# The u units of a gating stage: three 256-column products per weight block, or one of 512 columns and one of 256

## The reference

```python
def chunked_sgu(h, w_in, ln_g, ln_b, w_s, b_s, w_out):
    z = jax.nn.gelu(h @ w_in)
    u, v = jnp.split(z, 2, axis=-1)
    v = layer_norm(v, ln_g, ln_b)
    v = v.reshape(B, nc, CHUNK, N_SGU_GROUPS, SGU_GROUP_DIM)
    ws = jnp.where(causal[None], w_s, jnp.zeros_like(w_s))
    sv = jnp.einsum("gts,bcsgd->bctgd", ws, v) + b_s.T[None, None, :, :, None]
    return (u * sv.reshape(B, S, SGU_HALF)) @ w_out
```

## Time and profile before

| what | value |
| --- | --- |
| times of three executions | 1108.13, 1108.94, 1110.29 us; median 1108.94 us |
| the profiled execution | 1108.64 us, span from first to last instruction 1106.5 us |
| PE busy | 1074.8 us (97%) |
| DVE, ACT, POOL busy | 781.8 us (71%), 642.5 us (58%), 96.8 us (9%) |
| chain that ended last | PE 86%, DVE 8%, ACT 3%, issue 2% |
| L173, L174, L175 with 256 columns | 1152 each |

### The profile page before, as it was taken

How to read it: one execution, slowest core, us unless ns; L and a number is a source line. 1 busy time by engine, 2 the same in 40 slices (tenths; PEclk the granted TensorE clock), 3 DMA queues, 4 the chain that set the end, 5 groups by cost and what they waited for, 6 DMA issues and landing times.

```text
span 1106.5 us, 20061 instructions
## 1 busy us (share of the span) xinstructions
PE 1074.8 (97%) x6870; PEld 949.7 (86%) x6870; DVE 781.8 (71%) x1331; ACT 642.5 (58%) x1158; POOL 96.8 (9%) x119
## 2 busy tenths in 40 slices
PE   8989999999999999999999999999999998999998
PEld 7967999999788998777999999899678887888886
DVE  6657877777654367886877777698779748666664
ACT  6658444444764855666444444677777747554443
POOL 0140111111010002220111111000100000000000
PEclk9999999999999999999999999999999999999999
DMA  9353665555366475442665555265212544555541
GB/s 340 103 197 113 224 195 184 197 190 191 114 247 199 125 228 171 153 152 77 213 203 190 189 192 190 77 221 180 96 39 71 175 155 154 190 188 190 190 152 38
DMA packets 51380, 185.06 MB, mean 167 GB/s; under 512 B 5728, under 2 KB 6240, under 8 KB 51328
## 3 DMA queue, kind: packets, MB, share of 16 engines
q1 hardware_dynamic: 49248, 178.28, 48.4%
q0 software_dynamic: 1504, 5.44, 1.4%
q10 hardware_dynamic: 576, 0.64, 0.2%
HBM read 183.29 MB, written 1.05 MB: 167 GB/s over the span
## 4 chain that ended last, share of the span: by engine, by line
PE 86%; DVE 8%; ACT 3%; issue 2%; DMA 0%; DVEq 0%; SPq 0%; ACTq 0%
PE ps L228 28%; PE ps L173 15%; PE ps L175 15%; PE ps L174 15%; PE ps L198 5%; DVE w_lo L156 3%; PE ps L200 2%; PE ps L1612 1%; ACT both L430 1%; DVE arena L815 1%; DVE both L436 1%; PE ps L750 1%; PE ps L734 1%; PE ps L721 1%; PE ps L1623 1%
## 5 line engine op out<-in xcount | busy, mean ns | idle before, releaser
L156 DVE TENSOR_TENSOR w_lo<-raw,w_hi 128x1024 fp32r<-128x1024 f32 x336 | 418.0, 1254 | 118.5 <-ACT w_hi L151 116.7
L151 ACT ACTIVATE w_hi<-raw 128x1024 fp32r<-128x1024 f32 x336 | 346.9, 1052 | 98.8 <-PE ps L175 51.3
L173 PE MATMUL ps<-both,w_hi 128*128 128x256 f32 x1152 | 328.0, 285 | 1.9 <-DVE both L436 0.9
L174 PE MATMUL ps<-both,w_hi 128*128 128x256 f32 x1152 | 326.2, 283 | 0.0
L175 PE MATMUL ps<-both,w_lo 128*128 128x256 f32 x1152 | 326.2, 283 | 0.0
L228 PE MATMUL ps<-w_hi,both 128*128 128x512 f32 x992 | 293.8, 396 | 7.3 <-DVE both L1197 3.3
L173 PEld LDWEIGHTS ps<-both,w_hi 128*128 128x128 f32 x1152 | 221.1, 192 | 6.2 <-issue 2.9
L174 PEld LDWEIGHTS ps<-both,w_hi 128*128 128x128 f32 x1152 | 221.2, 192 | 1.5
L175 PEld LDWEIGHTS ps<-both,w_lo 128*128 128x128 f32 x1152 | 221.1, 192 | 0.0
L228 PEld LDWEIGHTS ps<-w_hi,both 128*128 128x128 f32 x992 | 178.8, 188 | 45.6 <-DVE w_lo L156 4.3
L228 PE MATMUL ps<-w_lo,both 128*128 128x512 f32 x496 | 158.2, 392 | 0.0
(11 more groups left out here) (199 smaller groups left out, 1095.8 us busy)
## 6 DMA issues: line engine op xcount, KB each, us to landing
raw<-in_w SPq DMA_DIRECT2D x336, 512.0 KB, 3.4
row<-in_rows POOLq DMA_DIRECT2D x7, 512.0 KB, 4.2
x<-in_x SPq DMA_DIRECT2D x2, 512.0 KB, 4.4
out<-x SPq DMA_DIRECT2D x4, 256.0 KB, 2.1
misc<-in_misc POOLq DMA_DIRECT2D x1, 512.0 KB, 5.7
arena<-in_ws POOLq DMA_DIRECT2D x1, 512.0 KB, 7.7
tab<-in_tables POOLq DMA_DIRECT2D x1, 320.0 KB, 4.4
tab<-in_tables POOLq DMA_DIRECT2D x1, 256.0 KB, 4.6
```

The lines of the kernel that those rows point to most:

```text
L151: act.activation(w_hi[:, s, :], raw[:, s, :], ACT.Copy).then_inc(hi_done, 1)
L156: dve.tensor_tensor(w_lo[:, s, :], raw[:, s, :], w_hi[:, s, :].bitcast(F32), ALU.subtract).then_inc(lo_done, 1)
L173: pe.matmul(o, l_hi, r_hi, start=first, stop=False)
L174: pe.matmul(o, l_hi, r_lo, start=False, stop=False)
```

## The change

- `features_apart` takes the place of `features` for the 24 units of u. The ring is now of single units: unit m fills bank `UB = (7, 0, 3)[m % 3]`, so three banks hold three units.
- Behind each unit, ACT copies the bank's second half to the buffer `pad` (L1095), DVE adds it to the first half and writes the sum to `G_U` (L1161, counted by `u_summed`). PE takes the bank again after that sum. Behind each pair, DVE multiplies the two sums by `ROW` in `G_U` (L1167), and ACT applies the gelu in place there (L1099). The weight splits stand between these steps: ACT copy, hi, copy, hi, gelu; DVE add, lo, add, multiply, lo.
- The 12 squares are four, three, three and two, with pairs 0, 1 and 2 between them. The root and its table load follow the last two, then an explicit load of the gelu table, then pair 3. The normalisations vn of tiles 0 to 2 move behind pair 8, and their spatial matmuls on PE from ahead of unit 18 to ahead of unit 20.
- Output tile 0 no longer waits for all gelus: its first token tile (banks 0 and 1) waits for the sum of unit 22, its second (banks 2 and 3) for that of unit 23. On ACT the second `high` stands before pair 11, on DVE the second `low` too.

```diff
-    UB = (7, 0, 1)
+    UB = (7, 0, 3)
...
-        for p in range(3):
-            if p == 1:
-                pe.wait_ge(g_sem.v, 2 * SGC)
-            for k in range(2):
-                features(pe, N_SGU + 2 * p + k, ps[:, UB[p], k * SEQ:(k + 1) * SEQ])
-        def later_pair(p, i=0):
-            pe.wait_ge(g_sem.u, p - 2 + 3 * i)
-            for k in range(2):
-                features(pe, N_SGU + 2 * p + k, ps[:, UB[p % 3], k * SEQ:(k + 1) * SEQ], i)
...
+        def u_unit(m, i=0):
+            if m in (1, 2):
+                pe.wait_ge(g_sem.v, 8)
+            if m >= 3:
+                pe.wait_ge(g_sem.u_summed, m - 2 + 6 * i)
+            features_apart(pe, N_SGU + m, UB[m % 3], i)
...
-        out_tile(0)
+        pe.wait_ge(g_sem.lo, 1)
+        for tt in range(TT):
+            pe.wait_ge(g_sem.u_summed, SGT - 1 + tt)
+            accumulate(pe, N_SGO, s_slot(0), True, False, tiles=(tt,))
...
         def pair(p, i, split):
-            split(0)
+            for k in range(2):
+                m = 2 * p + k
+                act.wait_ge(unit_used, N_SGU + m + 1 + 6 * i)
+                if m >= 2:
+                    act.wait_ge(g_sem.u_summed, m - 1 + 6 * i)
+                act.activation(pad[:, k, 2:2 + SEQ], ps[:, UB[m % 3], SEQ:2 * SEQ], ACT.Copy).then_inc(g_sem.u_part, 1)
+                split(k)
             act.wait_ge(g_sem.u_scaled, p + 1 + 3 * i)
-            dst = G_U[:, 2 * p:2 * p + 2, :] if isinstance(i, int) else G_U[:, bass.ds(2 * p + 6 * i, 2), :]
-            act.activation(dst.rearrange("p a b -> p (a b)"), ps[:, UB[p % 3], :],
-                           ACT.Gelu_apprx_tanh).then_inc(g_sem.u, 1)
-            split(1)
+            u = u_pair(p, i).rearrange("p a b -> p (a b)")
+            act.activation(u, u, ACT.Gelu_apprx_tanh).then_inc(g_sem.u, 1)
...
-        moments(0)
+        moments(0, 4)
         straight_pair(0)
-        moments(1)
+        moments(4, 7)
         straight_pair(1)
+        moments(7, 10)
+        straight_pair(2)
+        moments(10, 2 * SGC)
         act.wait_ge(g_sem.stat, 4)
         act.activation(lns[:, L_ROOT:L_ROOT + 2], lns[:, L_VAR:L_VAR + 2], ACT.Sqrt).then_inc(g_sem.root, 1)
-        act.wait_ge(g_sem.stat, 6)
-        for j in range(3):
-            vn(j)
-        straight_pair(2)
+        act.preload_act_table(ACT.Gelu_apprx_tanh)
...
-        def pair_row(p, i=0):
-
-            dve.wait_ge(unit_used, N_SGU + 2 * p + 2 + 6 * i)
-            uv = ps[:, UB[p % 3], :].rearrange("p (k t) -> p k t", k=2)
-            dve.tensor_tensor(uv, uv, ROW.rearrange("p (a t) -> p a t", a=1).to_broadcast([P, 2, SEQ]),
+        def pair_row(p, i=0, split=lambda j: None):
+            for k in range(2):
+                m = 2 * p + k
+                dve.wait_ge(g_sem.u_part, m + 1 + 6 * i)
+                dve.tensor_tensor(u_one(m, i), ps[:, UB[m % 3], 0:SEQ], pad[:, k, 2:2 + SEQ],
+                                  ALU.add).then_inc(g_sem.u_summed, 1)
+                if k == 0:
+                    split(0)
+            dve.wait_ge(g_sem.u_summed, 2 * p + 2 + 6 * i)
+            u = u_pair(p, i)
+            dve.tensor_tensor(u, u, ROW.rearrange("p (a t) -> p a t", a=1).to_broadcast([P, 2, SEQ]),
                               ALU.mult).then_inc(g_sem.u_scaled, 1)
+            split(1)
```

More of the change, by code:

```diff
@@ L971, in build @@
     L_SUM, L_SQ, L_TOT, L_NEG, L_VSUM, L_VAR, L_ROOT, L_INV, L_SHIFT = 0, 12, 24, 26, 28, 30, 32, 34, 36
-    g_sem = signals("sgu", "v u u_scaled masked rows rows_out stat square root vn mixed affine gated product hi lo")
-    UB = (7, 0, 1)
+    g_sem = signals("sgu", "v u u_part u_summed u_scaled masked rows rows_out stat square root vn mixed affine gated product hi lo")
+    UB = (7, 0, 3)
     VB = ((0, 3), (4, 5), (1, 2))
@@ L1010, in sgu_pe @@
             sgu_v_pe(pe, c)
-        for p in range(3):
-            if p == 1:
-                pe.wait_ge(g_sem.v, 2 * SGC)
-            for k in range(2):
-                features(pe, N_SGU + 2 * p + k, ps[:, UB[p], k * SEQ:(k + 1) * SEQ])
-        def later_pair(p, i=0):
-            pe.wait_ge(g_sem.u, p - 2 + 3 * i)
-            for k in range(2):
-                features(pe, N_SGU + 2 * p + k, ps[:, UB[p % 3], k * SEQ:(k + 1) * SEQ], i)
-        with pe.Fori(0, SGT // 6 - 2) as i:
-            for p in range(3, 6):
-                later_pair(p, i)
-        pe.wait_ge(next_sems.row_out, 2)
-        for j in range(3):
-            sgu_spatial(pe, j)
-        for p in range(SGT // 2 - 3, SGT // 2):
-            later_pair(p)
-        pe.wait_ge(g_sem.u, SGT // 2)
+        def u_unit(m, i=0):
[4 more added lines that the diff above has]
+            features_apart(pe, N_SGU + m, UB[m % 3], i)
+        for m in range(6):
+            u_unit(m)
+        with pe.Fori(0, SGT // 6 - 2) as i:
+            for m in range(6, 12):
+                u_unit(m, i)
+        for m in range(SGT - 6, SGT):
+            if m == SGT - 4:
+                for j in range(3):
+                    sgu_spatial(pe, j)
+            u_unit(m)
         def out_tile(j, i=0):
@@ L1070, in sgu_act, with moments @@
             hi_to(act, N_SGV + 4 * c + 9)
-        def moments(tt):
+        def moments(begin, end):
             act.wait_ge(g_sem.stat, 2)
-            for c in range(SGC):
-                if tt or c:
-                    act.wait_ge(g_sem.square, SGC * tt + c)
+            for n in range(begin, end):
+                tt, c = n // SGC, n % SGC
+                if n:
+                    act.wait_ge(g_sem.square, n)
                 act.activation(G_PR[:, 0:2, :].rearrange("p a b -> p (a b)"), G_V[:, tt, c * 512:(c + 1) * 512],
@@ L1123, in sgu_act @@
         act_at[0] = N_SGO
+        act.wait_ge(g_sem.stat, 6)
+        for j in range(3):
+            vn(j)
         for p in range(SGT // 2 - 3, SGT // 2):
             straight_pair(p)
-            if p == SGT // 2 - 3:
-                high(0)
+            if p < SGT // 2 - 1:
+                high(p - SGT // 2 + 3)
         vn(3)
-        high(1)
         with act.Fori(0, 3) as i:
@@ L1159, in sgu_dve @@
                           ALU.mult).then_inc(g_sem.stat, 1)
-        pair_row(0)
-        lo_to(dve, N_SGU + 7)
-        pair_row(1)
-        lo_to(dve, N_SGU + 9)
+        pair_row(0, 0, lambda j: lo_to(dve, N_SGU + 6 + j))
+        pair_row(1, 0, lambda j: lo_to(dve, N_SGU + 8 + j))
+        pair_row(2, 0, lambda j: lo_to(dve, N_SGU + 10 + j))
         dve.wait_ge(g_sem.square, 12)
@@ L1202, in sgu_dve @@
             for p in range(3, 6):
-                pair_row(p, i)
-                for k in range(2):
-                    lo_of(dve, N_SGU + 2 * p + 6 + k, i)
+                pair_row(p, i, lambda j, p=p: lo_of(dve, N_SGU + 2 * p + 6 + j, i))
         dve_at[0] = N_SGO
@@ L1214, in sgu_dve @@
         lo_to(dve, N_SGO + 3)
+        low(1)
         pair_row(11)
         lo_to(dve, N_SGO + 5)
-        low(1)
         with dve.Fori(0, 3) as i:
```

6 lines of the change are left out of this document (4 added, 2 removed).

## The result

| | before | changed |
|---|---|---|
| median | 1109.78 us (11 runs) | 1111.8 us (11 runs) |
| lowest to highest | 1108.13 to 1111.54 us | 1110.89 to 1114.66 us |
| profiled execution | 1108.64 us, span 1106.5 | 1110.94 us, span 1109.2 |
| unit 0 to output tile 0 | 72.02 us | 74.65 us |

The account below looks back on a forecast made before the run. PE was taken to bound the squares' stage, ACT just behind. Matmuls -1.75, ring +5.0, end -0.9 and restarts +0.3 gave +2.65 us, so 1111.6 us, 0.24% slower; range 1108.6 to 1113.8 us.

Parts of the forecast that it names:

- The bound: Squares' stretch, first 16.9 us: PE busy without a gap bounds it, ACT busy 15.91 us with 1 us to spare.
- The matmuls: 24 units of u on PE: 2.81 us per unit instead of 2.883, -1.75 us; bounds 0 to 2.5 us.
- The ring: PE waits for sums behind ACT's chain ahead of units 5, 7 and 9, none after: +5.0 us.
- The rule of the Trainium skill: Isolated matmul takes N/2.4 + 2.5 ns, so a unit of u goes from 2.62 to 2.60 us.
- The normalisations: Six ACT activations moved behind pair 8 cost nothing: done by 420.8, PE needs them at 421.5, cover 0.7 us.
- The end: Ahead of output tile 0: wait of 1.58 us becomes 0.7, behind the sum of unit 22; -0.9 us.
- The restarts: First matmuls after three new standstills of PE: 0.1 us each, +0.3 us, bounds 0 to 0.6.
- The sum: All terms over the kernel: +2.65 us, forecast 1111.6 us, 0.24% slower.
- The ring that holds: Rival at unit 9's release: unit 6's sum done by 385.6, nothing lost, -2.65 us, 1106.3 us; chance 0.11.
- half a loss: Rival: ACT's late chain shorter or partly absorbed by DVE's slack in the output loop, 1109.1 to 1110.6 us; chance 0.15.
- the rival: Clock falls to 1.2 GHz after PE's standstill ahead of unit 9: 3 to 6 us more, 1115 to 1118; chance 0.07.

Follow-up runs that it names:

- two experiments: Changed kernel with squares in two groups of six: 1112.2 us, ratio 1.0021; six-bank version with all of it, spatial matmuls ahead of unit 18: 1108.86 us, ratio 0.9988.

## Why the prediction was right, and where it was not

**The bound.** PE with ACT 1 us behind it: right. The reader should note that ACT's busy share in the squares' stretch fell, while ACT became what PE waits for.

**The matmuls, -1.75 us: too large.** The form is worth 1.29 us over the 24 units (69.19 us before, 67.90 in the kernel with six banks). The step that failed is the duration of the new unit, 2.81 us, read from a unit that stands alone between two output tiles in the MLP. Here too the first unit takes 2.81 us (360.75 to 363.56), but those that follow a unit take 2.83 (363.56 to 366.39); before it was 2.88. The rule of the Trainium skill that the prediction set beside it ("TensorE: Matmul & The Clock Gate", back-to-back issue gap) came, as an estimate, to about 0.5 us for the 24 units; the measured 1.29 lies between rule and row.

**The ring, +5.0 us: right, by its own steps.** From the first square to PE's start of unit 9 the chain was forecast as 26.1 us (364.5 to 390.6) and took 26.27 (364.91 to 391.18); a pair as 4.2 us and took 4.21; the tables as 2.8 and took 2.81 (387.25 to 390.06). The pieces came as forecast, ahead of units 5, 7 and 9, and none behind. Six banks take them away: unit 9 is then 5.00 us earlier. The restart of unit 9 comes on top (it takes 2.93 us, 2.82 with six banks). Two of the steps had been taken from rows with operands in PSUM: the multiplication out of SBUF took 0.69 us, as in the earlier trace rows, and the gelu 0.64 for 0.58 to 0.60. Units 20 to 23 win 0.2 us back against six banks (11.18 us for 11.38, by a pace of 2.77 us), so that the ring costs the units 4.90 us: they take 72.80 us (360.75 to 422.37 and 423.63 to 434.81) for the 67.90 with six banks, the spatial matmuls left out on both sides.

**The normalisations, nothing: right.** They run on ACT from 419.36 for 2.41 us, and the spatial matmuls follow 0.6 us behind them, at 422.37, when unit 19 ends; a cover of 0.7 us had been forecast:

```profile
419.36 2.41 ACT L1107 ACTIVATE arena<-arena,lns 128x128 f32<-128x128 f32 x6
```

The cover is there because the ring delays PE. With six banks PE comes before the last normalisation is done, and the same place in the order costs 0.35 us.

**The end, -0.9 us: right.** 1.58 to 0.59 us is 0.99. The sum of unit 22 is what is late, as forecast, a tenth earlier. The experiment with this part alone adds that it is worth 0.6 to 0.9 us in the kernel before.

**The restarts, +0.3 us.** They are in the 4.90 us of the ring, which the forecast had as 5.3 with them: the idle time is 4.4 us, and each restart and its first matmul (0.49 for 0.40 us) bring the rest.

**The sum.** -1.29 + 4.90 - 0.99 = +2.62 us, and 2.63 measured for the stage, against the forecast's +2.65. Two errors of 0.4 to 0.5 us, one in the form and one in the ring with its restarts, were of opposite sign and cancel; that is luck, and the time is closer than the terms deserve. The absolute time is luck too: the forecast of 1111.6 us starts from the 1108.94 us of three executions, and eleven give 1109.78, so that the two medians differ by 2.0 us only, and the ratio says 2.4.

**The rivals.** The ring that holds is out, and so is half a loss. The clock did not fall in the changed kernel's trace. But two experiments (standstills of 3.23 us and 2.05 us) show it falling in this stage, so the rival had a real mechanism; only its price of 3 to 6 us was wrong. The step that failed was to let the clock stay low for one or two units at half pace: it stayed low for about 3.4 us and cost 1.4 and 1.7 us.

**The change as a whole.** Each of its parts on PE's side is a gain or free with three banks: form, end, normalisations. The ring of three single units turned all of it into a loss, because it ties each bank's release to an ACT queue that has 25 us of squares, splits, gelus and tables in front of it (364.91 to 390.06). With six banks the same change is worth -1 us in the stage; with the order of ACT and DVE put right as well, -3.1.

## What to carry to other kernels

When a buffer's release moves to another engine, follow that engine's whole queue from its first item to the release, at rows' prices, and compare the end with when the buffer is wanted: busy shares showed ACT relieved (15.91 to 13.99 us of 16.9) just when it became the bound. A gain on PE counts only up to the next thing that ends last; here the matmul form's 1.29 us vanished in front of the normalisations and of DVE's `low` and sum until those were moved too. And the duration of a repeated unit is read from one that follows its like, not from one that stands alone.
